# Norms in the scale of later units, projections first, stage ends tile by tile, and gathers for two experts at once, in a two-layer trunk on one core

## The chip, the cores and the metric

One core of one Trainium2 chip. Its engines: TensorE (PE) with its weight loads (PEld), VectorE (DVE), ScalarE (ACT), GpSimd (POOL), SyncE (SP), which issues the DMAs here. The metric is the device time of one execution in microseconds, lower is better.

## The reference, cut to what matters

256 tokens of 1024 float32 values pass two layers. Each layer adds a token mixer and a channel mixer, each behind a root-mean-square norm with a gain; a last norm follows.

```python
h = rmsnorm(x, ln_attn[l])            # x * rsqrt(mean(x*x) + 1e-6) * gain
x = x + token_mixer(h, ...)           # concat[ attention | conv | retention ] @ w_out
h = rmsnorm(x, ln_ffn[l])
x = x + swiglu(h, w13, w2)            # layer 0: (silu(h@A) * (h@B)) @ w2, D_FF = 2816
x = x + moe_ffn(h, router, w13, w2)   # layer 1: top 2 of 8 experts, each such a swiglu
out = rmsnorm(x, ln_final)
```

The token mixer projects h to 2840 columns: queries, keys and values of a three-branch attention (compressed, selected, window; 8 heads of 64), its gates, a 31-tap causal convolution of 256 channels, and a retention of 4 heads. With 256 tokens all blocks are selected, so the selected and the window branch are causal attention over all keys.

## The kernel before, in words

Tokens lie on the partitions in two tiles of 128 (`i` = 0, 1); x stays in SBUF. Weights come through a ring of three slots (`SLOTS`, 24 KB per partition each) by SP, in a fixed order: eight items per mixer, then 11 items of the dense swiglu or 88 of the experts (8 experts x 11 steps of 256 hidden columns). SP waits, before each, until the slot's last reader is done (`LAST_READ`), and its DMAs go out in program order. Each engine runs its own straight program; semaphores order them. The PSUM has eight banks; in a mixer they are handed out in turn by `GROUP`, and `full` and `freed` wait for a bank's use.

**Norm** (`rms_squares` L884, `rms_apply` L1133). ACT squares both tiles with row sums, DVE makes mean + eps, ACT takes the root, DVE the reciprocal and x times it (`xn`), PE transposes `xn` in 16 blocks, DVE multiplies the gain in while copying to `hT`. All that follows waits for it. It comes five times: twice per layer, once at the end.

**Mixer** (`MIXER` L81; the order that PE, ACT and DVE all follow). After the norm: q, ks (window and selected keys), kcv (compressed), vsw (values and gates), cg and ca (convolution gate and input), rqk and rvg (retention). Each projection stage is 16 fp32 matmuls of 128x128 by 256 (32 instructions) or as much in other shape. They stand between the twelve attention units: score k, then probT of k-1 (four transposes), then pv of k-2. For a score DVE takes the row maximum, ACT the exponential; ACT copies probT; DVE scales pv. Other stages in between: conv 0 to 7 (DVE multiply-adds of about four taps each), hid, hidT, cmpkv, cscore, cprobT, cpv (compressed branch), retT, rets, reto (retention). At the end: attn_sum (DVE adds the branches), convT with the layer norm on DVE, retnorm, convB, conv_pw, retcat, and the output product in four groups of (column half, tile): "out" has the first 4 of 8 row blocks, "out_rest" the others; DVE adds each to x.

**Swiglu in three products** (`three`). Each fp32 operand is split in a high part in fp32r (ACT copy, `hi_up`, `hi_down`) and a low rest (DVE subtraction, `lo_up`, `lo_down`), and three matmuls of 512 columns are summed. Per step: four weight pieces for up (`up`), two for down (`down`). Step J: up pieces 0 and 1, turn of step J-1 (transposes of the gated hidden values), up 2 and 3, down of J-1. `hidden` is silu on ACT and the product on DVE, `turned` the split of the transposed values. One buffer holds the four up and two down pieces (`wh`, `wl`), so a piece is split again when PE has read it.

**Experts.** Per expert: `picks` makes a 0/1 matrix token x slot on DVE; `gather` multiplies x (three bf16 parts, 48 matmuls of 128 columns) with it, `picked` scales by the gain and splits (8 ACT and 8 DVE operations), 11 steps, `summed` splits the result, `pick_turned` and `scatter` bring it back to the tokens, `scattered` adds it to x with the gate (4 DVE operations). For expert e > 0 gather stands in step 7 of the expert before, picked in step 10; of the expert before, summed and scatter in step 1, scattered in step 2. Ahead stand the router's logits, `routing` (rank and choice) and the bf16 parts of x. A second round exists for over 128 tokens of an expert, behind a branch; it does not run with this input. After the branch the last norm and the output follow.

Of the kernel before, what the change touches and what calls it, by code (L numbers as in the profile page):

```python
# [7 lines left out]
F32 = mybir.dt.float32  # L8
# [7 lines left out]
P = 128  # L16
# [32 lines left out]
MIX_FILLS = [len([m for m in range(len(MIX_ITEMS)) if m % SLOTS == s]) for s in range(SLOTS)]  # L49
ROUND = EXPERTS * STEPS  # L50


def fills(steps, s):

    return len(range(s, steps, SLOTS))
# [15 lines left out]
for _name, _n in (("ln_attn", KD), ("ln_ffn", KD), ("pe", 2 * 16), ("conv_w", NC * CONV_K), ("conv_b", NC),  # L71
# [10 lines left out]
    ("norm", 0), ("q", 0), ("q", 1), ("ks", 0), ("score", 0), ("kcv", 0), ("score", 1), ("probT", 0), ("vsw", 0),  # L82
    ("score", 2), ("probT", 1), ("pv", 0), ("cg", 0), ("score", 3), ("probT", 2), ("pv", 1), ("ca", 0),
    ("conv", 0), ("score", 4), ("probT", 3), ("pv", 2), ("rqk", 0), ("conv", 1), ("score", 5), ("probT", 4),
    ("pv", 3), ("rqk", 1), ("conv", 2), ("score", 6), ("probT", 5), ("pv", 4), ("hid", 0), ("conv", 3), ("retT", 0),
    ("score", 7), ("probT", 6), ("pv", 5), ("hid", 1), ("conv", 4), ("retT", 1), ("hidT", 0), ("score", 8),
    ("probT", 7), ("pv", 6), ("rvg", 0), ("conv", 5), ("hidT", 1), ("rets", 0), ("score", 9),
    ("probT", 8), ("pv", 7), ("cmpkv", 0), ("conv", 6), ("cscore", 0), ("score", 10), ("rvg", 1), ("probT", 9),
    ("pv", 8), ("rets", 1), ("score", 11), ("probT", 10), ("pv", 9), ("conv", 7), ("cprobT", 0),
    ("probT", 11), ("pv", 10), ("reto", 0), ("pv", 11), ("cpv", 0), ("cpv", 1), ("attn_sum", 0), ("attn_sum", 1),  # L90
    ("convT", 0), ("out", 0), ("retnorm", 0), ("convB", 0), ("out", 1), ("retcat", 0), ("conv_pw", 0),
    ("out_rest", 0), ("out_rest", 1), ("norm", 1)]


PSUM_GROUPS = {"norm": 4, "q": 1, "ks": 1, "score": 1, "kcv": 1, "cg": 1, "ca": 1, "probT": 1, "vsw": 2, "pv": 1,
               "rqk": 1, "rvg": 1, "hid": 1, "hidT": 1, "cmpkv": 1, "retT": 1, "cscore": 2, "rets": 2,
               "cprobT": 1, "reto": 1, "cpv": 1, "convT": 1, "convB": 1, "attn_sum": 1, "conv_pw": 1, "retcat": 1, "out": 2,
               "conv": 0, "retnorm": 0, "out_rest": 0}
BANKS = 8
SCATTER = ((6, 7), (2, 3))  # L100

# [1529 lines left out]
```

## Time and profile before

| | |
|---|---|
| median of 3 runs | 1409.85 us (1407.54 to 1415.88) |
| span of the profiled execution | 1413.9 us (the profile has no other time for it) |
| PE busy | 1317.7 us (93%), 6346 matmuls |
| DVE busy | 989.8 us (70%) |
| ACT busy | 841.6 us (60%) |
| POOL busy | 0.2 us |
| mean DMA rate | 253 GB/s over the span, 337 to 365 in the experts |
| chain of waits | 84% PE, 10% DVE, 3% ACT |

Stages by the timeline: first norm to 15.5, mixer 0 to 185.3, norm to 202, dense swiglu to 394.7, sum and norm to 406.6, mixer 1 to 571, norm and routing to 602, experts to 1397.7, end 1413.9. Times count from the first instruction. An fp32 matmul is two instructions in the profile. The granted clock of PE is 1.00 at 2.4 GHz and 0.50 at 1.2 GHz.

### The profile page before, as it was taken

The numbers are of one execution on the slowest core, as the hardware profiler recorded it, in microseconds if no ns is written. First come the engines' busy times: TensorE is split into PE (matmuls) and PEld (weight loads), VectorE is DVE, ScalarE is ACT, GpSimd is POOL, SyncE is SP. The second block draws the span as 40 slices with busy tenths as digits, with TensorE's granted clock in tenths as the row PEclk, the third lists the DMA queues.
The fourth block names the chain that finished last, engine by engine and source line by source line (L and its number), as shares of the span: only waits on it lengthen the run. The fifth ranks groups of instructions, "written<-read, shape, count | busy, mean of one in ns | idle before, by whom it ended". The sixth has DMA issues, their size and how long they took to land.

```text
span 1413.9 us, 15866 instructions
## 1 busy us (share of the span) xinstructions
PE 1317.7 (93%) x6346; PEld 1056.7 (75%) x6346; DVE 989.8 (70%) x1115; ACT 841.6 (60%) x1181; POOL 0.2 (0%) x4
## 2 busy tenths in 40 slices
PE   6999969999879999699999999999999999999994
PEld 5876548888768764578888888888788788888883
DVE  2275445455322674588898998998998988989993
ACT  2324235444213252387877877887887778778782
POOL 0000000000000000000000000000000000000000
PEclk9998979999979999699999999999999999999998
DMA  8231184552232311769889889989898898898860
GB/s 328 89 133 40 79 327 179 186 197 94 101 140 90 133 62 65 320 249 379 321 352 373 336 350 347 361 342 351 341 369 344 330 385 325 353 380 332 338 263 32
DMA packets 32176, 357.63 MB, mean 253 GB/s; under 512 B 3681, under 2 KB 3809, under 8 KB 4705
## 3 DMA queue, kind: packets, MB, share of 16 engines
q1 hardware_dynamic: 32096, 356.55, 64.4%
q8 instruction: 52, 0.85, 0.2%
q14 instruction: 28, 0.22, 0.0%
HBM read 355.49 MB, written 1.05 MB: 252 GB/s over the span
## 4 chain that ended last, share of the span: by engine, by line
PE 84%; DVE 10%; ACT 3%; issue 1%; DMA 0%; DVEq 0%; ACTq 0%
PE ps L480 81%; DVE wl L1356 4%; PE ps L483 3%; DVE x L1480 1%; DVE hTl L1459 1%; ACT xn L888 1%; ACT wh L1000 1%; ACT hTh L1057 1%; DVE arena L1159 0%; ACT L890 0%; DMA x<-x_in 0%; ACT arena L932 0%; DVE arena L1370 0%; DVE wl L1363 0%; DVE xn L1140 0%
## 5 line engine op out<-in xcount | busy, mean ns | idle before, releaser
L1356 DVE TENSOR_TENSOR wl<-ring,wh 128x2048 fp32r<-128x2048 f32 x198 | 452.9, 2288 | 57.7 <-ACT wh L1000 50.4
L1000 ACT ACTIVATE wh<-ring 128x1024 fp32r<-128x1024 f32 x396 | 419.5, 1061 | 79.1 <-PE ps L480 74.5
L480 PE MATMUL ps<-wh,hTh 128*128 128x512 f32 x880 | 352.6, 401 | 15.2 <-DVE wl L1356 7.6
L480 PE MATMUL ps<-wh,hTl 128*128 128x512 f32 x880 | 345.3, 392 | 0.0
L480 PE MATMUL ps<-wl,hTh 128*128 128x512 f32 x880 | 344.6, 392 | 0.0
L1363 DVE TENSOR_TENSOR wl<-ring,wh 128x2048 fp32r<-128x2048 f32 x99 | 226.6, 2288 | 70.0 <-ACT wh L1010 68.5
L1010 ACT ACTIVATE wh<-ring 128x1024 fp32r<-128x1024 f32 x198 | 209.5, 1066 | 87.1 <-PE ps L480 82.3
L480 PEld LDWEIGHTS ps<-wh,hTh 128*128 128x128 f32 x880 | 165.9, 189 | 51.5 <-DVE hTl L1387 8.0
L480 PEld LDWEIGHTS ps<-wh,hTl 128*128 128x128 f32 x880 | 165.6, 188 | 35.5
L480 PEld LDWEIGHTS ps<-wl,hTh 128*128 128x128 f32 x880 | 166.1, 189 | 32.5
L480 PE MATMUL ps<-wh,gTh 128*128 128x512 f32 x440 | 174.3, 396 | 7.5 <-DVE gTl L1377 7.5
L480 PE MATMUL ps<-wh,gTl 128*128 128x512 f32 x440 | 172.3, 392 | 0.0
L480 PE MATMUL ps<-wl,gTh 128*128 128x512 f32 x440 | 172.2, 391 | 0.0
L480 PEld LDWEIGHTS ps<-wh,gTh 128*128 128x128 f32 x440 | 83.4, 190 | 24.7 <-DVE wl L1363 7.9
L480 PEld LDWEIGHTS ps<-wh,gTl 128*128 128x128 f32 x440 | 83.2, 189 | 17.7
L480 PEld LDWEIGHTS ps<-wl,gTh 128*128 128x128 f32 x440 | 83.5, 190 | 16.8
L480 PE MATMUL ps<-hT,ring 128*128 128x256 f32 x384 | 86.8, 387 | 2.0 <-DVE hT L1184 2.0
L932 ACT ACTIVATE arena<-ps,arena 128x128 f32<-128x128 f32 (+1 forms) x64 | 26.2, 418 | 98.7 <-DVE arena L1224 97.9
L480 PEld LDWEIGHTS ps<-hT,ring 128*128 128x128 f32 x384 | 73.9, 194 | 12.9 <-issue 2.8
L483 PE MATMUL ps<-cst,arena 128*128 128x128 f32 x376 | 65.0, 278 | 10.6 <-ACT arena L932 6.4
L480 PE MATMUL ps<-ring,hT 128*128 128x256 f32 (+2 forms) x256 | 74.1, 447 | 0.0
L1025 ACT ACTIVATE gTh<-ps 128x256 fp32r<-128x256 f32 x110 | 41.6, 388 | 54.6 <-PE ps L483 54.6
(160 smaller groups left out, 1004.6 us busy)
## 6 DMA issues: line engine op xcount, KB each, us to landing
ring<-moe_in SPq DMA_DIRECT2D x88, 2048.0 KB, 8.7
ring<-moe_in SPq DMA_DIRECT2D x88, 1024.0 KB, 8.7
ring<-ffn_in SPq DMA_DIRECT2D x11, 2048.0 KB, 7.5
ring<-mix_in SPq DMA_DIRECT2D x6, 3072.0 KB, 10.1
ring<-ffn_in SPq DMA_DIRECT2D x11, 1024.0 KB, 7.2
ring<-mix_in SPq DMA_DIRECT2D x4, 2048.0 KB, 10.7
ring<-mix_in SPq DMA_DIRECT2D x2, 2368.0 KB, 9.1
ring<-mix_in SPq DMA_DIRECT2D x2, 2176.0 KB, 8.5
```

Of the source, the lines that this page charges most:

```text
L480: return nc.tensor.matmul(o, lhsT, rhs, start=first, stop=last, skip_group_check=True)
L483: return nc.tensor.transpose(o, a, ident)
L888: A(xn[:, i, :], x[:, i, :], ACT.Square, accum_out=stat[:, 0, i:i + 1]).then_inc(s_ss, 1)
L932: last = A(prob[:, k % 3, c * keys:(c + 1) * keys], bank(l, stage, k)[:, c * keys:(c + 1) * keys], ACT.Exp, bias=nmax[:, k, c:c + 1], scal ...
L1000: A(wh[:, p, :], ring[:, J % SLOTS, p * PIECE:(p + 1) * PIECE], ACT.Copy).then_inc(s_hi, 1)
L1010: A(wh[:, UP + c, :], ring[:, J % SLOTS, (UP + c) * PIECE:(UP + c + 1) * PIECE], ACT.Copy)\
L1025: A(gTh[:, i, :, :], ps[:, b, 0:FC].rearrange("p (c t) -> p c t", c=DOWN), ACT.Copy)\
L1057: last = A(hTh[:, c, 0:P], ps[:, 6 + half, q * P:(q + 1) * P], ACT.Copy, scale=param(1, "ln_ffn")[:, c:c + 1])
L1356: V.tensor_tensor(wl[:, w, :], raw, wh[:, w, :].bitcast(F32), ALU.subtract).then_inc(s_lo, 1)
L1363: V.tensor_tensor(wl[:, w, :], raw, wh[:, w, :].bitcast(F32), ALU.subtract).then_inc(s_lo, 1)
L1459: last = V.scalar_tensor_tensor(out=hTl[:, c, 0:P], in0=ps[:, 6 + c // 4, (c % 4) * P:(c % 4 + 1) * P], scalar=param(1, "ln_ffn")[:, c:c + ...
L1480: V.scalar_tensor_tensor(out=xs, in0=ps[:, SCATTER[i][n], :], scalar=gate[:, i, e:e + 1], in1=xs, op0=ALU.mult, op1=ALU.add).then_inc(s_xa ...
```

## The change

- **Dense swiglu's norm goes to the scale of later units.** `hT` for it is transposed from x itself (`xT`, per column half and tile); the factor 1/rms enters as the scale of ACT's silu and of DVE's product in `hidden`. ACT squares (now half tiles, `square`, `root`) run after the mixer, and ACT and DVE wait for the result before dense step 1's pieces. The router's logits come from unscaled x likewise (`logits`), scaled where the softmax is taken.
- **Projections first in a mixer.** The new `MIXER` has stat, nT (norm and transposes per tile), vsw, rqk, rvg, cg, ca, kcv, q, ks ahead of unit 0, with conv 0 to 4 beside them; the twelve units follow with conv 5 to 7 and the rest between. The weight items load in that order (`LOADS`), the first in two DMAs of half. `asum` makes half of each attn_sum earlier; the convolution's layer norm (`cnorm`) comes after both attn_sums.
- **Stage ends tile by tile.** In the mixer's tail `pre` splits the up pieces of the next stage's step 0. The last dense step finishes tile 0 first, sums it, and transposes it between the last products of tile 1; `wh`, `wl` become `whU`, `whD`, `wlU`, `wlD`, and the last step's down pieces go to the up buffers. The end of the experts is done by halves and tiles, in both arms of the branch.
- **Gathers for two experts at once.** x is split in two fp32r parts (ACT, and GpSimd for the rest, no bf16), `pick` is 256 slots wide: 32 matmuls of 256 columns in step 7 of odd experts. picked comes in step 1 (odd) or step 8 (even expert), scatter in step 2, scattered in step 3. `pick_turned` transposes fp32.
- GpSimd also does the memsets. Waits for the low down pieces and for `gTl` stand ahead of each group of three matmuls (`down_part`).

```diff
+    ("stat", 0), ("nT", 0), ("stat", 1), ("vsw", 0), ("nT", 1), ("vsw", 1), ("rqk", 0), ("rqk", 1), ("rvg", 0), ("rvg", 1),
+    ("cg", 0), ("ca", 0), ("conv", 0), ("kcv", 0), ("retT", 0), ("conv", 1), ("q", 0), ("retT", 1), ("conv", 2),
+    ("q", 1), ("conv", 3), ("ks", 0), ("conv", 4),
+    ("score", 0), ("hid", 0), ("score", 1), ("probT", 0), ("rets", 0),
+    ("score", 2), ("probT", 1), ("pv", 0), ("hid", 1), ("conv", 5),
+    ("score", 3), ("probT", 2), ("pv", 1), ("rets", 1), ("hidT", 0), ("hidT", 1),
+    ("score", 4), ("probT", 3), ("pv", 2), ("reto", 0), ("conv", 6),
+    ("score", 5), ("probT", 4), ("pv", 3), ("cmpkv", 0),
+    ("score", 6), ("probT", 5), ("pv", 4), ("cscore", 0), ("conv", 7),
+    ("score", 7), ("probT", 6), ("pv", 5), ("score", 8), ("probT", 7), ("pv", 6), ("cprobT", 0),
...
+    ("asum", 1), ("probT", 11), ("pv", 10), ("convT", 0), ("pv", 11), ("attn_sum", 1), ("cnorm", 0), ("out", 0),
+    ("retnorm", 0), ("convB", 0), ("pre", 0), ("out", 1), ("retcat", 0), ("conv_pw", 0), ("pre", 1),
+    ("out_rest", 0), ("out_rest", 1), ("out_rest", 2), ("xT", 0), ("xT", 1), ("out_rest", 3), ("xT", 2), ("xT", 3)]
...
+                J = STEPS - 1
+                for c in range(DOWN):
+                    for n in range(2):
+                        down_part(DENSE, J - 1, 0, c, n)
+                turn(DENSE, J)
+                for n in range(2):
+                    last = down_part(DENSE, J - 1, 1, 0, n)
+                last.then_inc(s_piece, 1)
+                for n in range(2):
+                    for c in range(DOWN):
+                        last = down_part(DENSE, J, 0, c, n)
+                    last.then_inc(s_ysum, 1)
+                for n in range(2):
+                    last = down_part(DENSE, J - 1, 1, 1, n)
+                last.then_inc(s_piece, 1)
+                for n in range(2):
+                    for c in range(DOWN):
+                        last = down_part(DENSE, J, 1, c, n)
+                    last.then_inc(s_ysum, 1)
+                    if n == 0:
+                        norm_turned(1, 0)
...
+            def down_part(f, J, i, c, n):
+                pe.wait_ge(s_lo, f.down_pair(J) + 1)
+                pe.wait_ge(s_gTl, f.unit(J, i) + 1)
+                w = slice(n * 512, (n + 1) * 512)
+                return three(ps[:, 4 + 2 * i + n, :], g_high(f, J, i)[:, c, :], g_low(f, J, i)[:, c, :], ...)
...
+                for c in range(KD):
+                    b = GATHER[c // 2]
+                    for i in range(NT):
+                        if ex == 0:
+                            pe.wait_ge(s_xl, i + 1)
+                        for part, src in enumerate((xh, xl)):
+                            last = mm(ps[:, b, (c % 2) * 2 * P:(c % 2 + 1) * 2 * P], src[:, i, c * P:(c + 1) * P],
+                                      pick[:, i, :], i == part == 0, i == NT - 1 and part == 1)
...
+                    A(silu[:, i, :], ps[:, up_bank(f, J, i), 0:FC], ACT.Silu,
+                      scale=stat[:, 3, i:i + 1] if f is DENSE else 1.0).then_inc(s_silu, 1)
...
+            for i in range(NT):
+                pool.wait_ge(s_xh, i + 1)
+                if i:
+                    pool.wait_ge(s_xl, i)
+                G.tensor_tensor(xl[:, i, :], xn[:, i, :], xh[:, i, :].bitcast(F32), ALU.subtract).then_inc(s_xl, 1)
```

## Rows read from the trace of the kernel before

**Rows 1.** Windows: stretch, length, busy by engine (instructions), PE clock, DMA share, GB/s.
```profile
15.50:98.90 83.40, 80.91 (x440) 69.82 (x440) 27.61 (x76) 19.24 (x50) 0.00 (x0) 1.00 0.42 165
98.90:185.30 86.40, 80.05 (x358) 48.18 (x358) 46.47 (x120) 30.80 (x69) 0.00 (x0) 0.90 0.20 75
185.30:202.00 16.70, 3.67 (x16) 3.27 (x16) 11.92 (x15) 9.65 (x14) 0.00 (x0) 0.62 0.96 391
...
406.60:492.00 85.40, 83.09 (x440) 71.36 (x440) 27.43 (x75) 19.22 (x49) 0.00 (x0) 0.97 0.24 88
492.00:572.00 80.00, 72.22 (x358) 43.77 (x358) 47.18 (x121) 30.70 (x70) 0.00 (x0) 1.00 0.22 84
...
698.60:797.50 98.90, 98.03 (x478) 80.33 (x477) 88.67 (x72) 78.75 (x100) 0.00 (x0) 1.00 0.90 351
```

**Rows 2.** Chain of work that ended last: start, length in us, what.
```profile
0.73 5.28 DMA x<-x_in
...
15.55 20.97 PE ps L480 x96
...
65.90 8.78 PE ps L480 x45
...
202.02 18.60 PE ps L480 x72
221.06 16.37 PE ps L480 x72
...
372.26 10.94 PE ps L480 x48
...
557.09 13.98 PE ps L480 x32
...
675.17 8.21 PE ps L480 x36
...
709.53 10.03 PE ps L480 x44
...
1401.41 2.78 issue
```

**Rows 3.** Timeline of DVE in mixer 1: start, length, line, operation, [idle before].
```profile
513.20 3.62 DVE L1159 SCALAR_TENSOR_TENSOR arena<-hc,par,arena 128x256 f32<-128x256 f32 x8
516.86 0.61 DVE L1268 SCALAR_TENSOR_TENSOR arena<-ps,cst 128x64 f32<-128x64 f32 x4
...
520.57 0.68 DVE L1222 TENSOR_REDUCE arena<-ps 128x2 f32<-128x512 f32 x1
```

**Rows 4.** Timeline of PE in both mixers.
```profile
100.53 1.08 PE L483 MATMUL ps<-cst,arena 128*128 128x128 f32 x4 [2.59 <-ACT arena L932]
...
493.81 0.63 PE L483 MATMUL ps<-cst,arena 128*128 128x128 f32 x4 [2.59 <-ACT arena L932]
...
538.36 1.06 PE L483 MATMUL ps<-cst,arena 128*128 128x128 f32 x8 [0.70 <-DVE arena L1343]
```

**Rows 5.** Timeline of PE from routing to the first expert.
```profile
581.19 6.97 PE L480 MATMUL ps<-router,hT 128*128 128x8 f32 x32 [0.87 <-DVE hT L1184]
...
597.58 5.03 PE L480 MATMUL ps<-pick,xb 128*128 128x128 bf16 x48 [4.26 <-DVE pick L1450]
...
602.41 0.47 PE L480 MATMUL ps<-wh,hTh 128*128 128x512 f32 x1
```

**Rows 6.** Timeline of PE and DVE in the second expert's stretch.
```profile
666.55 2.85 PE L480 MATMUL ps<-pick,xb 128*128 128x128 bf16 x48
...
696.02 2.16 DVE L1459 SCALAR_TENSOR_TENSOR hTl<-ps,par,hTh 128x128 fp32r<-128x128 f32 x8 [0.29 <-ACT hTh L1057]
...
723.39 2.72 DVE L1480 SCALAR_TENSOR_TENSOR x<-ps,arena,x 128x512 f32<-128x512 f32 x4
```

**Rows 7.** Timeline of PE and DVE at the end.
```profile
1391.02 0.76 PE L480 MATMUL ps<-wh,gTh 128*128 128x512 f32 x1 [3.68 <-DVE gTl L1377]
...
1408.18 2.48 DVE L1144 SCALAR_TENSOR_TENSOR xn<-x,stat,gfin 128x1024 f32<-128x1024 f32 x2
```

More of the change, by code:

```diff
@@ L81 @@
 MIXER = [
[L82 to L91, printed above, removed]
@@ L1094, in experts, with final, final_norm @@
                         A(pickT, ps[:, 3, 0:T].rearrange("p (i t) -> p i t", i=NT), ACT.Copy).then_inc(s_sptc, 1)
-                    hi_down(f, J, 0)
-                    hi_down(f, J, 1)
-                turned(f, ROUND - 1)
-                summed(f, first + EXPERTS - 1)
+                    if j == 8 and ex % 2 and e < EXPERTS - 1:
+                        picked(ex + 1)
+                    if not last:
+                        hi_down(f, J, 0)
+                        hi_down(f, J, 1)
+                turned(f, ROUND - 1)
+            def final(rnd):
+                f = MOE[rnd]
+                ex = rnd * EXPERTS + EXPERTS - 1
+                act.wait_ge(s_yhalf, rnd + 1)
+                A(yeh[:, 0, :], ps[:, 4, :], ACT.Copy).then_inc(s_yeh, 1)
+                act.wait_ge(s_piece, f.end())
+                A(yeh[:, 1, :], ps[:, 5, :], ACT.Copy).then_inc(s_yeh, 1)
+            def final_norm(rnd):
+                ex = rnd * EXPERTS + EXPERTS - 1
+                for i in range(NT):
+                    for h in range(2):
+                        act.wait_ge(s_xadd, 4 * ex + 1 + 2 * i + h + 1)
+                        square(4, i, h)
+                    root(4, i)
             mixer(0)
@@ L1388, in dense @@
+                for i in range(NT):
+                    rstd(1, i).then_inc(s_rstd, 1)
+                dve.wait_ge(s_rstd, NT)
                 for J in range(STEPS):
@@ L1495, in experts @@
                     ex = first + e
+                    last = J == ROUND - 1
                     if j == 1 and e:
-                        summed(ex - 1)
+                        for n in range(2):
+                            summed(ex - 1, n)
                     if J:
                         turned(f, J - 1)
-                    if J < ROUND - 1:
+                    if not last:
                         lo_up(f, J + 1, 0)
-                    if j == 2 and e:
-                        scattered(ex - 1)
@@ L1504, in experts @@
-                    if j == STEPS - 1 and e < EXPERTS - 1:
+                    if j == 3 and e:
+                        for n in range(2):
+                            for i in range(NT):
+                                scattered(ex - 1, i, n)
+                    hidden(f, J)
+                    if not last:
+                        lo_up(f, J + 1, 1)
+                    if j == 1 and ex % 2 == 0:
                         picked(ex + 1)
-                    hidden(f, J)
-                    if J < ROUND - 1:
-                        lo_up(f, J + 1, 1)
```

1040 lines of the change are left out of this document (617 added, 423 removed).

## The prediction

> **What bounds the kernel now.** Read the windows first [rows 1]: in every stage TensorE (PE) is busy nearly all the time, in one expert's stretch 98.03 of 98.90 us, at full clock. What is left is in three places: the stretches between stages (185.3 to 202, some 20 us before 406.6, 571 to 602, and the end), the low clock behind each of them, and some 9 to 10 us of idle PE inside each mixer (83.40 - 80.91 + 86.40 - 80.05 = 8.8 us in layer 0, 2.3 + 7.8 = 10.1 us in layer 1). The chain of waits second [rows 2]: it is PE almost throughout, and it leaves PE only at those boundaries, where it goes through the norm (ACT squares, square root, VectorE (DVE) scaling, transposes, DVE copies). The timelines third [rows 3 to 7]: they give the durations. So the change can gain at boundaries, lose inside the mixers, and touch the expert loop only by the gathers and by where DVE's extra work falls.
>
> The profile has no time of its own for the profiled execution beyond its span, 1413.9 us; the three timed runs are 1407.5 to 1415.9, median 1409.85. I sum against 1413.9 and take off 4.05 at the end.
>
> **Start.** Now x (1 MB) lands at 6.0 (0.73 + 5.28 [rows 2]), norm and transposes of both tiles follow, and the first projection starts at 15.55. New: half of x goes first. About 2 us of the 5.28 are latency, so tile 0 is there at about 4.3; squares 1.4, table load and square root 1.5, reciprocal and scaling 1.0, eight transposes 1.9 with the first copy under them, last copy 0.8: the first projection starts near 10.95. It needs only half of the first weight item (1 MB in place of 3 MB). Tile 1's transposes and copy (1.1 + 1.0) now lie after it. Net 15.55 - 10.95 - 2.1 = **2.5 gained** (bounds 0 to 5). Later weight items come in the order of use; each projection stage is 6.99 us (20.97 / 3), so none is late.
>
> **Inside a mixer.** The PE work is the same. Before, projections (7 us each) stood between the attention units, so a unit's reduce, exp and copy were always covered: 8.78 us for 45 matmuls at 65.90 [rows 2] is one projection and most of a unit, which alone costs PE about 2.2 us. Now all projections come first, and the twelve units run back to back, with DVE also doing the last convolution parts (3.62 each [rows 3]). I walked the new order. Worst place: cscore, conv 7, score 7. DVE's cscore takes 3.7 us (516.86 to 520.57), conv 7 3.6, the reduce of unit 7 0.9 and its exp 1.0: 9.1 us after PE finished cscore, and PE has only score 7, probT 6, pv 5, score 8 in front of probT 7, about 3.3 us: 5.8 idle. Before, rvg (7 us) covered it. Next: conv 4 ahead of unit 0's reduce 1.9, conv 6 1.6, unit 3 0.3, the copy of the keys 1.5 (as before), the sums and copies ahead of "out" 3.5 (before 2.7 to 3.4, since half of the sum is now done early), 0.8 in "out". Together 16 us idle against 8.8 and 10.1. An idle of 5.8 us is longer than those behind which the clock fell: after 2.59 of waiting PE went on at full clock at 493.81 in layer 1 and at half at 100.53 in layer 0 (four transposes 0.63 and 1.08 [rows 4]). That shows in rows 1: the same 358 matmuls are busy 80.05 us at a granted 0.90 in layer 0 and 72.22 at 1.00 in layer 1, 7.8 us for nothing. I charge 2 us per mixer for the clock. Layer 0: -7.2 - 2 + 7.8 = **-1.4**. Layer 1: -5.9 - 2 = **-7.9**. Bounds: idle as before (+14 in all) to another 8 each (-16).
>
> **First mixer to dense.** Before: PE's last output matmul ends at 185.3, the dense ups start at 202.02: 16.7 us with 3.67 of transposes [rows 1], and then 72 matmuls take 18.60 in place of 16.37 [rows 2] from a granted clock of 0.5 (1.2 of 2.4 GHz; the mean over the gap is 0.62). New: the squares and the root are off this path (the scale enters after the up matmuls), weight pieces of step 0 are split during "out", and x is transposed raw, half by half: transposes 2.1 in all, 0.3 of waiting. Half 1's low part is ready 3 us behind the first up, which has 5.5 us of half 0 first. 16.7 - 2.4 + 2.2 = **16.5**. What is late next: ACT does four squares, roots and a wait before it splits step 1; its first DVE piece is ready about 10.1 us after the first up and wanted at 10.9. That cover is 0.8 us; if it is gone, it costs 1 to 3.
>
> **Dense to second mixer.** The last ups end at 377.4 (half of the 48 matmuls from 372.26 [rows 2]); the projections start at 406.6, and their matmuls are 83.09 busy where layer 0's equal 440 are 80.91: 29.2 + 2.2 = 31.4. New: the last down weights are split into the up buffers, so the wait for DVE at 384 to 387 goes; the order is 12 matmuls, turn 0.5, 6, 12, 6, 6, then transposes of tile 0 between the last two groups. At 0.228 each these 48 matmuls take 10.9; sum, squares, root and scaling of tile 0 (4.2 us after its second half) end at 387.8, 0.3 late; vsw of tile 0 starts at 390.3, and tile 1 (1.1 + 0.9) follows. 31.4 - 12.9 - 2.0 = **16.5**.
>
> **Second mixer to experts.** Before: 571.07 to 602.41, 31.3 us. New, from the last output matmul: two first logit halves 2.1, transposes 1.0, copy, two second halves 2.0, so logits at 5.5 in place of 17 (the old 32 took 6.97 at half clock [rows 5]). Selection 2.2 (fewer links), rank 0.5 in bf16, DVE's leftovers and the rank copy 0.9, four picks of 0.3: gather at 9.9. PE is idle most of 5.5 to 9.9, so its clock will be low: the old first gather ran 48 in 5.03 [rows 5] at half clock, against 2.85 later, and the clock rose about at its end. The new one has 32 matmuls of 256 columns: 0.213 each at half clock for 5 us, 0.13 for the rest, 6.1. First up at 16.0, plus 1.06 for the two earlier transposes: **14.2 gained** (bounds 9 to 18). GpSimd's two subtractions have no row in this trace: DVE's equal one is 1.22; up to 3.8 for the second is hidden, since its input is there at 6.1 and the picks end at 9.9. I take 2.4, twice DVE; at 6 us it would cost 2.2. By the Trainium skill, GPSIMD Engine Reference, Engine selection, a two-input elementwise operation should not go to GpSimd, about 2x slower; its 4497 ns for 2048 columns would make this an estimate of 2.2 us, still hidden. No row here shows it.
>
> **Expert loop.** Before, from 602.41 to the last ups: per expert 98.9 [rows 1], made of 11 x 8.434, gather 2.8 (48 matmuls [rows 6]), scatter 1.82 (10.03 - 8.21 [rows 2]), pick transposes 0.19, stalls 1.3. New: three gathers in the loop of 32 matmuls in place of seven of 48. The pace of a matmul with 128 fp32 weight columns is 0.13 us (8 in 1.06 [rows 4]), above the 0.107 that 256 columns stream: 4.1 each. 19.6 - 12.3 = 7.3. Bounds for it: 0.114 (half of the 512-column pace) to 0.218 (fp32): +1.5 to -8.5. Here the Trainium skill (TensorE: Matmul & The Clock Gate, Weight-path perf modes) speaks against the change: fast weight load is for weights that aren't fp32, so the gather gives it up; its load time of 107 ns is an estimate of 3.4 per gather, 2 us better in all than my 4.1. Pick transposes in fp32: -0.6. Stalls: DVE's pieces are 7.7 of each 8.43, and its results are some 1.9 us ahead of need, so an inserted piece stalls PE by what goes over 1.9. Before, picked (2.16 [rows 6]) at the last step, summed (1.3) and scattered (2.72) within three steps: 1.3 per expert. New, even experts: summed and picked at step 1, 0.8; scattered at step 3, 1.3; odd ones about 0.1: 1.1 per expert. In all 11.7 to 8, 3.6. Sum **10.3** (bounds 0 to 15). DMA: a step wants 3.15 MB per 8.43 us, 373 GB/s, windows reach over 400; no bound.
>
> **The end.** Before, the last down starts at 1391.02 at half clock (0.76 the first) behind 3.68 idle [rows 7], and 1401.41 to 1404.2 is the branch [rows 2]; then norm and output of both tiles. New: last down weights split early, down at 1387.9 at full clock, ends 1390.7; the branch (about 3.4 on ACT and DVE) runs beside it; yeh and yel by halves to 1393.0, scatter, four sums to 1395.9, tile 0's norm beside them, last product at 1400.1, output 3.2 (1413.9 less the last product's end, 1410.7 [rows 7]). Ends at 1403.3: **10.6** (bounds 6 to 13).
>
> **Sum.** 2.5 - 1.4 + 16.5 + 16.5 - 7.9 + 14.2 + 10.3 + 10.6 = 61.3. 1413.9 - 61.3 - 4.05 = 1348.5; the forecast is **1348**.
>
> **Rivals.** (A) Forecast, 1348, own range 1338 to 1358. (B) The mixer's units stay covered: idle as before, clock kept, 14 less: 1334. For it: the page's DVE is busy only 27.6 of 83.4 us in the first half of a mixer; against: the count at cscore. (C) The opposite: twelve bare units, each with reduce, exp and copy in series, wait 0.7 more each, or the gather runs at the fp32 pace: 16 or 9 more, 1357 to 1370. (D) The norm work is not hidden but moved: ACT's squares hold up dense step 1, and the first expert steps wait for DVE, so two of the three boundary gains are halved: 1365. (E) Slower: the down matmuls now carry two waits for each three matmuls. That is 6 more per expert step and 14 more per dense step, 88 x 6 + 11 x 14 = 682. From 0.09 us each the gain is gone; at 0.12, 1430. Against: 36 matmuls with six met waits take 8.21, 72 with six take 16.37, the same pace, so a met wait costs under 0.01.
>
> **Chances.** A 0.50, B 0.20, C 0.17, D 0.08, E 0.03, 0.02 for something between. Range 1328 to 1371: B and most of C and D lie in it. A measurement of this kernel tells 0.5% (7 us) from no change. Faster 0.96, same 0.01, slower 0.03.
>
> **What would show it.** Dense ups at about 185 and at full clock; second mixer's first projection near 371, first expert up near 560; one PE idle of 5 to 6 us behind cscore in each mixer; 32-matmul gathers of about 4 us every other expert; the last down at full clock with no idle before it. I am wrong if the clock stays low in the bare units, if PE waits at dense step 1 by more than 3 us, or if a pair of experts isn't 1.5 to 3 us shorter than 197.8.

## The result and the profile after

The changed kernel takes 1376.63 us (median of 4 runs, 1375.6 to 1380.82), the kernel before 1411.03 us on the same chip (1407.54 to 1415.88): ratio 0.976, 95% interval 0.973 to 0.978. It is faster by 34 us, where 61 were forecast, and lies 5.6 us above the range. The profiled execution of after is its slowest run, 1380.82 us with a span of 1379.0; the span of before is 1413.9, so the two traces differ by 34.9 us.

The first fence is the timeline of TensorE (PE) after (start, length, line, shapes, count, in brackets the idle time before and who ended it); it holds the marks that the prediction named at the stage boundaries.

```profile
199.71 0.48 PE L555 MATMUL ps<-whU,hTh 128*128 128x512 f32 x1
386.75 4.01 PE L555 MATMUL ps<-ring,hT 128*128 128x280 f32 x16 [0.40 <-PE ps L555]
535.62 9.96 PE L555 MATMUL ps<-ring,arena 128*128 128x512 f32 x16 [0.73 <-issue]
580.85 0.21 PE L555 MATMUL ps<-selb,beforeb 128*128 128x8 bf16 x2 [5.26 <-DVE selb L1670]
582.75 0.58 PE L555 MATMUL ps<-pick,xh 128*128 128x256 f32 x1 [1.60 <-DVE pick L1695]
```

With these starts and those of before, each stage can be set against the prediction's terms. The terms are its own, put together by stage; of the 7.8 us of low clock that it takes back from before in layer 0, 1.2 are counted in "out", whose first 16 matmuls took 8.30 us there in place of 7.1. Their sum is its 61.3.

| stretch | before | after | measured | predicted |
|---|---|---|---|---|
| start to "out" of layer 0 | 152.65 | 163.20 | +10.6 | +0.1 |
| "out" to first dense up | 49.4 | 36.5 | -12.9 | -15.5 |
| dense, to the second mixer's first projection | 204.6 | 187.0 | -17.5 | -18.7 |
| second mixer to its "out" | 133.1 | 148.9 | +15.7 | +7.9 |
| "out" to first expert up | 62.7 | 52.3 | -10.4 | -14.2 |
| experts and end | 811.5 | 791.1 | -20.4 | -20.9 |
| sum | | | -34.9 | -61.3 |

The reader is to see that boundaries, experts and end came within about 1.5 us each, leaving aside "out", and that the two mixers and their "out" hold 24.2 of the missing 26.4 us. Windows over the mixers say how (length, busy time of PE, weight loads, DVE, ACT and POOL with instructions, granted clock of PE, share of the DMAs, GB/s). Before, first projection to "out", both layers:

```profile
15.55:152.65 137.10, 129.21 (x719) 103.20 (x719) 62.78 (x172) 44.93 (x111) 0.00 (x0) 0.95 0.34 133
406.59:539.72 133.13, 124.76 (x718) 100.87 (x719) 62.97 (x173) 44.71 (x111) 0.00 (x0) 0.98 0.24 91
```

After, the same stretches, then the unit phases alone:

```profile
11.13:163.20 152.07, 137.65 (x726) 111.90 (x727) 67.14 (x183) 37.52 (x107) 0.00 (x0) 0.91 0.37 148
386.75:535.62 148.87, 134.10 (x727) 109.74 (x727) 66.90 (x182) 38.28 (x109) 0.00 (x0) 0.92 0.25 95
99.00:163.20 64.20, 52.40 (x344) 45.35 (x345) 37.52 (x111) 28.01 (x89) 0.00 (x0) 0.78 0.19 76
468.00:535.60 67.60, 55.33 (x390) 47.39 (x391) 41.76 (x120) 28.02 (x89) 0.00 (x0) 0.82 0.24 94
```

Idle time of PE rose from 7.9 and 8.4 us to 14.4 and 14.8 (length less busy). The busy time of nearly the same work rose by 8.4 and 9.3 us, only 1.04 of it for the eight transposes of tile 1 that moved into the stretch. The granted clock of the unit phase is 0.78 and 0.82, a mix of 1.2 and 2.4 GHz, where layer 1 before had 1.00 [rows 1]. (At the very start of an execution the column is no guide: layer 0's first 16 matmuls after take 6.28 us where layer 1's take 4.01, and the clock shown there is 1.00.) The timeline of layer 1's units shows where the clock fell:

```profile
492.83 1.05 PE L555 MATMUL ps<-arena 128*128 128x128 f32 x8
496.16 0.63 PE L558 MATMUL ps<-cst,arena 128*128 128x128 f32 x4 [2.28 <-ACT arena L1084]
496.93 5.41 PE L555 MATMUL ps<-arena 128*128 128x64 f32 x40
502.46 1.92 PE L555 MATMUL ps<-arena 128*128 128x256 f32 x4
...
511.71 1.09 PE L558 MATMUL ps<-cst,arena 128*128 128x128 f32 x4 [3.64 <-ACT arena L1084]
527.05 1.32 PE L558 MATMUL ps<-cst,arena 128*128 128x128 f32 x8 [1.48 <-DVE arena L1561]
533.79 1.09 PE L558 MATMUL ps<-cst,arena 128*128 128x128 f32 x4 [1.37 <-DVE arena L1561]
545.86 7.03 PE L555 MATMUL ps<-ring,arena 128*128 128x512 f32 x16
```

Four transposes take 0.63 us at full clock and 1.09 at half: behind the wait of 2.28 they are still fast, the 40 short matmuls that follow are not (5.41 us; 2.97 at full clock in the run with dummies at two waits), nor the scores (four in 1.92 instead of 1.03) and the transposes behind 3.64. Windows from 496 on place the fall about a microsecond behind the end of the wait:

```profile
496.00:496.80 0.80, 0.63 (x4) 0.42 (x4) 0.80 (x2) 0.62 (x2) 0.00 (x0) 1.00 0.94 369
496.80:498.00 1.20, 1.07 (x6) 1.10 (x6) 0.59 (x4) 0.77 (x5) 0.00 (x0) 0.58 0.99 423
498.00:500.00 2.00, 2.00 (x16) 1.88 (x17) 0.29 (x1) 1.34 (x6) 0.00 (x0) 0.50 1.07 451
500.00:502.30 2.30, 2.30 (x23) 2.26 (x24) 0.00 (x0) 0.00 (x0) 0.00 (x0) 0.50 0.95 406
```

It is back at full for units 9 to 11 and lost again at the sums. "Out" itself, long matmuls without a gap, takes 9.96 us for its first 16 and 7.03 for the next. In layer 0 the same first 16 take 10.14. The DVE timeline beneath the longest wait (cscore, the eighth part of the convolution, then unit 7's reduce):

```profile
502.37 0.61 DVE L1484 SCALAR_TENSOR_TENSOR arena<-ps,cst 128x64 f32<-128x64 f32 x4 [3.16 <-PE ps L555]
...
506.08 3.63 DVE L1381 SCALAR_TENSOR_TENSOR arena<-hc,par,arena 128x256 f32<-128x256 f32 x8
509.62 0.68 DVE L1439 TENSOR_REDUCE arena<-ps 128x2 f32<-128x512 f32 x1
```

PE finishes cscore at 502.3 and is released at 511.7, 9.4 us later; the prediction had 9.1. So the walk through the new order was right. What was not is the pace at which PE works beside it.

### The profile page after: what moved, and what is told of

The parts are those of the page before. It is cut to its first block, busy times and chain, and to the rows that moved or that the text cites. A ratio compares the mean times of both kernels' runs of the same rounds, so it can differ in the third digit from the quotient of the medians.

```text
span 1379.0 us, 15726 instructions
## 1 busy us (share of the span) xinstructions
PE 1314.9 (95%) x6085; PEld 1054.9 (76%) x6085; DVE 986.9 (72%) x1117; ACT 830.7 (60%) x1194; POOL 8.5 (1%) x12
## 3 DMA queue, kind: packets, MB, share of 16 engines
HBM read 355.49 MB, written 1.05 MB: 259 GB/s over the span
## 4 chain that ended last, share of the span: by engine, by line
PE 87%; DVE 9%; ACT 2%; issue 1%; DMA 0%; DVEq 0%; ACTq 0%
PE ps L555 83%; PE ps L558 4%; DVE wlU L1593 3%; DVE x L1723 1%; DVE arena L1381 1%; ACT arena L1084 1%; ACT whU L1170 1%; DVE arena L1439 0%; DVE wlD L1600 0%; DVE xn L1357 0%; DMA x<-x_in 0%; DVE arena L1561 0%; DVE arena L1408 0%; DVE hT L1365 0%; ACT gTh L1196 0%
## 5 line engine op out<-in xcount | busy, mean ns | idle before, releaser
L1593 DVE TENSOR_TENSOR wlU<-ring,whU 128x2048 fp32r<-128x2048 f32 x198 | 453.2, 2289 | 75.6 <-ACT whU L1170 72.2
L1170 ACT ACTIVATE whU<-ring 128x1024 fp32r<-128x1024 f32 x396 | 418.5, 1061 | 65.2 <-PE ps L555 60.7
L555 PE MATMUL ps<-whU,hTh 128*128 128x512 f32 x880 | 352.8, 401 | 4.2 <-DVE wlU L1593 4.2
L555 PE MATMUL ps<-whU,hTl 128*128 128x512 f32 x880 | 344.9, 392 | 0.0
L555 PE MATMUL ps<-wlU,hTh 128*128 128x512 f32 x880 | 343.1, 390 | 0.0
L1600 DVE TENSOR_TENSOR wlD<-ring,whD 128x2048 fp32r<-128x2048 f32 x97 | 222.1, 2289 | 51.7 <-ACT whD L1182 51.7
L1182 ACT ACTIVATE whD<-ring 128x1024 fp32r<-128x1024 f32 x194 | 205.3, 1065 | 74.9 <-PE ps L555 69.5
L555 PE MATMUL ps<-whD,gTh 128*128 128x512 f32 x428 | 168.1, 393 | 0.4 <-DVE gTl L1618 0.4
L555 PE MATMUL ps<-whD,gTl 128*128 128x512 f32 x428 | 167.4, 391 | 0.0
L555 PE MATMUL ps<-wlD,gTh 128*128 128x512 f32 x428 | 166.6, 389 | 0.0
L558 PEld LDWEIGHTS ps<-cst,arena 128*128 128x128 f32 x376 | 52.3, 151 | 41.3 <-issue 26.9
L555 PEld LDWEIGHTS ps<-hT,ring 128*128 128x128 f32 x384 | 72.6, 190 | 10.6 <-issue 1.0
```

The costliest lines, as they stand in the source:

```text
L555: return nc.tensor.matmul(o, lhsT, rhs, start=first, stop=last, skip_group_check=True)
L558: return nc.tensor.transpose(o, a, ident)
L1170: A(whU[:, p, :], ring[:, f.slot(J), p * PIECE:(p + 1) * PIECE], ACT.Copy).then_inc(s_hi, 1)
L1182: A(wh_down(f, J, c), ring[:, f.slot(J), (UP + c) * PIECE:(UP + c + 1) * PIECE], ACT.Copy)\
L1593: V.tensor_tensor(wlU[:, w, :], raw, whU[:, w, :].bitcast(F32), ALU.subtract).then_inc(s_lo, 1)
L1600: V.tensor_tensor(wl_down(f, J), raw, high.bitcast(F32), ALU.subtract).then_inc(s_lo, 1)
```

## The experiments

Theory 1: the mixers lose by the clock, which falls because PE waits between short units. Theory 2: they lose by the idle time itself, or the clock is low for the shape of the units' matmuls. Rivals: another part of the change. Times are medians of 4 runs (of 10 for the last one); "mixers" are the times from first projection to "out" in layer 0 and 1 of the profiled execution.

**Dummies in the waits.**

```diff
+ def spin(o, n):
+     for _ in range(n):
+         mm(o[:, 0:512].rearrange("p (n k) -> p n k", n=4), identb[:], spread(causalb[:], 1, 4), True, True)
  elif stage == "probT":
      o = begin(l, stage, k)
+     spin(o, {0: 8, 5: 9, 7: 15}.get(k, 0))      # and 6, 6, 5, 2 at score 0, the sums, out
      pe.wait_ge(s_exp, l * len(UNITS) + k + 1)
```

> The kernel after, with dummy bf16 matmuls of 512 columns (0.21 us each at full clock) put on TensorE just ahead of the waits of the unit phase: 6 ahead of unit 0's scores, 8, 9 and 15 ahead of the turns of units 0, 5 and 7, 6 and 5 ahead of the two attention sums, 2 ahead of the output projection (51 per mixer, each group no longer than the idle time it stands in; what they write is overwritten). Nothing else moves. Theory 1 (the loss in the mixers is mostly the clock: TensorE waits with nothing to do, then goes on at half clock; against before 8.5 and 9.3 us of the 15.0 and 15.7 are longer busy time): the granted clock from the first unit to the end of 'out' stays near 1.00, the two mixers take about 143 and 140 us in place of 152 and 149, the whole 1359 to 1363. Theory 2 (the loss is the idle time itself, and the clock is low there because the units' matmuls are narrow, whatever stands between them): the dummies change nothing or run at half clock themselves and overrun the gaps: 1377 to 1390.

Measured: 1360.21 us (1358.32 to 1360.75), ratio to before 0.962 (0.959 to 0.966); mixers 144.21 and 141.67. Its PE timeline at the end of layer 1's units, and its unit phase in a window:

```profile
516.27 0.66 PE L558 MATMUL ps<-cst,arena 128*128 128x128 f32 x4 [0.20 <-DVE arena L1570]
517.66 7.11 PE L555 MATMUL ps<-ring,arena 128*128 128x512 f32 x16 [0.30 <-issue]
457.45:517.66 60.21, 58.38 (x435) 44.85 (x436) 41.09 (x118) 27.80 (x89) 0.00 (x0) 0.94 0.27 107
```

No real work moved, and 16.4 us are gone from the median; "out" is at full clock. Between the two traces it is 21.0 us: the mixers stand 7.9 and 7.2 us lower, each "out" 3.0 and 2.9. So most of the loss is the clock, as theory 1 says, and filled waits keep it up. But the clock of the unit phase is 0.94 and not near 1.00, and the stretch that is left has no long wait ahead of it:

```profile
486.10 3.47 PE L555 MATMUL ps<-arena 128*128 128x64 f32 x40 [0.20 <-ACT arena L1103]
489.69 1.92 PE L555 MATMUL ps<-arena 128*128 128x256 f32 x4
```

From about 488.4 to 495.2 PE runs at half clock (the four scores in 1.92 us instead of 1.03), though in the 24 us before it waited only 0.24 and 0.20 us. In layer 0 the same happens at the same place, from about 126.6 on. The fall comes among the 40 short matmuls of the first row, which are 8 of 64 columns and then cscore's 32 of 16 columns; in the next run the same 40, behind the same dummies, stay at full clock in layer 1. So waits are not the only thing that brings the clock down, and whether short matmuls do it alone was not isolated.

**Dummies at two of the waits only** (9 and 15, units 5 and 7).

> The kernel after with 9 and 15 dummies ahead of the turns of units 5 and 7 only (2.28 and 3.64 us of waiting), none elsewhere. With dummies in all seven waits the whole fell by 17 us. If the clock is lost at these two waits only: nearly the same, 1360 to 1364. If any wait between short units costs it, it falls later, at the two sums ahead of 'out' (1.48 and 1.37 us), and the 16 matmuls of 'out' take about 10 us instead of 7.1: 1366 to 1370. If the two waits have nothing to do with it: 1377.

Measured: 1370.77 us (1363.27 to 1372.33), ratio 0.969 (0.965 to 0.974); mixers 146.08 and 146.38.

```profile
504.01 0.66 PE L558 MATMUL ps<-cst,arena 128*128 128x128 f32 x4 [2.71 <-ACT arena L1093]
517.03 1.94 PE L558 MATMUL ps<-cst,arena 128*128 128x128 f32 x8 [1.47 <-DVE arena L1570]
526.32 9.04 PE L555 MATMUL ps<-ring,arena 128*128 128x512 f32 x16 [0.84 <-issue]
```

The whole is 0.8 us above the second expectation. Units 5 to 9 keep the full clock, and it falls at the sums instead: eight transposes 1.94 us, "out" 9.04. Filling two of the waits gave 5.9 us of the 16.4. The row at 504.01 gives the idle of unit 7 at full clock: 15 dummies of 0.213 us and 2.71 are 5.9 us, the prediction's 5.8. After showed 3.64 only because PE worked at half clock through the 9.4 us of DVE and ACT, so part of the slow work lay where it would have waited.

**The old order of projections and units**, with its loads, in the new kernel.

```diff
- ("vsw", 0), ("nT", 1), ("vsw", 1), ("rqk", 0), ... ("q", 1), ("ks", 0), ("score", 0), ...
+ ("q", 0), ("q", 1), ("ks", 0), ("score", 0), ("kcv", 0), ("score", 1), ("probT", 0), ("vsw", 0), ...
- LOADS = ((2, ...), (3, ...), (1, ...), (0, ...), ...
+ LOADS = ((0, ...), (1, ...), (2, ...), (3, ...), ...
```

> The kernel after, with one part undone: inside the mixers the projections stand between the attention units again in the order of the kernel before (q first, so the first projection needs both token tiles), and the weight items are loaded in that order; the new boundaries, the norm after the up matmuls, the expert loop and the end stay. Theories 1 and 2 alike (the loss comes from the bare units): first projection to output projection takes 134 to 138 us in each mixer in place of 152.1 and 148.9, with the clock at 1.00 in layer 1; the boundaries ahead of the mixers lose 2 to 3 us each; whole 1350 to 1354. Rival (the loss comes from something else that the change brought into the mixers, as the split sums, the waits on banks or the loading of weights): the mixers stay near 149 to 152, whole 1377 to 1383.

Measured: 1369.22 us (1367.38 to 1372.02), ratio 0.969 (0.965 to 0.972); mixers 142.57 and 142.05. A miss of 15 us: half of the loss came back. It had kept the new end of the units, with the products of the compressed branch right behind their transposes. So that end was undone too:

```diff
- ("cpv", 0), ("cpv", 1), ("probT", 11), ("pv", 10), ("asum", 0), ("reto", 0), ("attn_sum", 0), ("asum", 1),
- ("convT", 0), ("pv", 11), ("attn_sum", 1),
+ ("probT", 11), ("pv", 10), ("reto", 0), ("pv", 11), ("cpv", 0), ("cpv", 1), ("asum", 0), ("asum", 1),
+ ("attn_sum", 0), ("attn_sum", 1), ("convT", 0),
```

> The kernel with the projections between the units again (the earlier run with the old order took 142 us in each mixer, not 134 to 138), now with the end of the units too in the order of the kernel before: products of units 10 and 11, then the sums of both tiles one after the other, then the transposes of the convolution. If the missing 7 us of that run came from its split sums (waits of 1.68, 1.67, 1.37 and 0.73 us, and the half clock behind them): mixers at 134 to 137, whole 1355 to 1360. If they came from elsewhere (the bare vsw stages ahead, the loads, the banks): no change, 1367 to 1371.

Measured: 1356.56 us (1356.42 to 1362.22), ratio 0.962 (0.957 to 0.967); mixers 133.25 and 138.11. Windows of the two kernels, layer 0, the first with the new end, the second with the old:

```profile
15.43:158.00 142.57, 132.07 (x718) 105.85 (x719) 64.67 (x178) 42.47 (x110) 0.00 (x0) 0.94 0.36 142
```

```profile
15.46:148.71 133.25, 124.70 (x718) 100.80 (x719) 63.23 (x175) 42.17 (x110) 0.00 (x0) 1.00 0.39 153
```

The same 718 matmuls are busy 132.07 and 124.70 us. The second is nearly the price of a mixer's work at full clock; only its first 96 matmuls took 23.12 us where layer 0 before took 20.96 (20.97 in [rows 2]), so the price is 122.5, and layer 1 before gives the same (124.76 less the 2.2 us of its slow first 96). The two steps bring 20.1 us together, 13 of them the second. But not all of the 13 is the order of the sums: in layer 0 the kernel with the new end had already lost 5.4 us to the other by cprobT, the last stage that both have in the same place, and 1.7 us in layer 1, over the same instructions and waits; its clock fell behind the wait of 2.60 in layer 0, the other's did not. Of the 9.3 and 3.9 us by which the mixers differ, 4.0 and 2.3 come behind the first stage that was moved. The rest is where the clock happened to fall.

**The convolution under the projections.** Here the projections stay first and the units bare; DVE's convolution leaves the unit phase, and for that cg and ca, with their weight item, come ahead of rqk.

```diff
- ("vsw", 1), ("rqk", 0), ("rqk", 1), ("rvg", 0), ("rvg", 1), ("cg", 0), ("ca", 0), ("conv", 0), ("kcv", 0), ...
+ ("vsw", 1), ("cg", 0), ("ca", 0), ("rqk", 0), ("conv", 0), ("rqk", 1), ("conv", 1), ("rvg", 0), ("conv", 2),
+ ("rvg", 1), ("conv", 3), ("retT", 0), ("kcv", 0), ("conv", 4), ... ("q", 1), ("conv", 6), ("conv", 7), ("ks", 0),
```

> The kernel after, with cg and ca moved ahead of rqk (and their weight item loaded second), so that all eight convolution parts run on VectorE under the projections and none in the unit phase. The projections still come first and the units still run bare. Theory 2 (VectorE's order makes the idle): the waits of TensorE for the exp of units 0, 5 and 7 (1.96, 2.28 and 3.64 us in layer 1) fall below 1 us each, 5 to 6 us of idle less in each mixer; if the clock then still falls in the units: 1364 to 1367. Theory 1 (it is the waits that bring the clock down): with fewer waits the clock stays up too and another 5 to 8 us per mixer come back: 1350 to 1356. Rival (each bare unit is a series of reduce, exp and copy that takes longer than TensorE's part of it): idle only moves from unit to unit, 1372 to 1378.

Measured: 1348.77 us (1347.94 to 1352.32), ratio 0.955 (0.952 to 0.959), 1.2 us below the range for theory 1. Its mixers:

```profile
11.15:145.24 134.09, 126.88 (x727) 102.98 (x727) 67.19 (x182) 37.43 (x107) 0.00 (x0) 0.99 0.42 167
367.25:503.94 136.69, 127.38 (x726) 104.12 (x727) 67.45 (x182) 38.31 (x109) 0.00 (x0) 0.96 0.27 104
```

Against after it is 27.9 us in the medians; in the traces 7.2 and 5.5 us less idle, 10.8 and 6.7 less busy for the same matmuls. The waits at the turns of units 0 and 5 are gone, that of unit 7 is 0.84 in layer 0 and 2.50 in layer 1:

```profile
126.67 0.63 PE L558 MATMUL ps<-cst,arena 128*128 128x128 f32 x4 [0.84 <-ACT arena L1084]
480.96 0.63 PE L558 MATMUL ps<-cst,arena 128*128 128x128 f32 x4 [2.50 <-ACT arena L1084]
```

The two are one and the same release. DVE and ACT let PE go 10.06 and 10.05 us after the start of unit 6's scores (116.61 and 470.91). In layer 0 the clock had fallen at about 121, and PE's own work ahead of the wait took longer (four scores 1.87 us, four transposes 1.06; in layer 1 1.03 and 0.60), which is the 1.66 us by which the wait is shorter. So half clock ahead of this wait costs nothing, since PE would have waited anyway. That fall, too, came with no wait since 94.39, right behind the same 40 short matmuls as in the run with dummies.

The bare units are thus no great fault by themselves: most of the clock is lost where PE waits, and DVE's order made the waits. What is left is at the sums (waits of 1.48 and 1.37) with "out" at 8.59 and 10.14 us.

**On top of it, one edit each.** The end of the units reordered, so that the convolution's transposes stand in the last wait:

```diff
- ("pv", 9), ("attn_sum", 0), ("asum", 1), ("probT", 11), ("pv", 10), ("convT", 0), ("pv", 11), ("attn_sum", 1),
+ ("pv", 9), ("asum", 1), ("probT", 11), ("pv", 10), ("pv", 11), ("attn_sum", 0), ("convT", 0), ("attn_sum", 1),
```

> The kernel with the convolution early, and one more edit: the products of units 10 and 11 come first, then the attention sum of tile 0, the transposes of the convolution (0.85 us), the sum of tile 1. If the waits of 1.48 and 1.37 us ahead of 'out' are real dependences that other work can cover: the first goes, the second falls to about 0.5, 2.4 us per mixer, and 'out' runs at full clock (7.1 in place of 8.6 and 10.1 us): 1338 to 1343. Rival: VectorE still works on units 10 and 11 whatever stands there, the waits only move: 1347 to 1350.

Measured: 1342.31 us (1340.77 to 1343.43), ratio 0.951 (0.946 to 0.955); mixers 133.44 and 134.77.

```profile
497.64 1.50 PE L558 MATMUL ps<-cst,arena 128*128 128x128 f32 x12 [1.14 <-DVE arena L1561]
499.88 7.11 PE L555 MATMUL ps<-ring,arena 128*128 128x512 f32 x16 [0.73 <-issue]
```

One wait of 1.14 us and one under 0.5 in place of 1.48 and 1.37, and "out" at full clock. Dummies in the remaining waits instead:

> The kernel with the convolution early, plus dummies of 0.21 us: 6 ahead of unit 0's scores, 4 ahead of unit 7's turn, 6 and 5 ahead of the two sums, 2 ahead of 'out' (23 per mixer, about 4.9 us, in gaps of 1.53, 0.84 or 2.50, 1.48, 1.37 and 0.73). Theory 1 (waits bring the clock down): the last stretches at half clock go, 1.5 us in layer 0 and 3 to 4 in layer 1, whole 1343 to 1346. If the clock is only lost in waits over 2 us: nothing, 1348 to 1350.

Measured: 1342.05 us (1339.56 to 1343.89), ratio 0.951 (0.946 to 0.955); mixers 134.14 and 132.42, "out" 7.1 in both. It gains slightly more than expected and as much as the reordering, which costs nothing. Among the waits that it filled only the one of 2.50 us was longer than 2, and in layer 0 there was none such, yet "out" came back to full clock there too: the waits of 1.48, 1.37 and 0.73 us ahead of it matter.

The end, with the branch's condition and the table for the square root loaded ahead:

```diff
+ act.wait_ge(s_over, 1)
+ more = act.value_load(over[0:1, 0:1], min_val=0, max_val=1)
  experts(0)
+ act.preload_act_table(ACT.Sqrt)
```

> The kernel with the convolution early, and the end changed: ScalarE and VectorE load the branch's condition before the experts, and the table for the square root is loaded ahead of the branch. After the last transposed unit the chain of the kernel after has 2.45 us of branch and 1.28 of table load on ScalarE, beside 4.3 us of last down matmuls. If that ScalarE chain ends last: 1 to 3 us less, 1346 to 1348, and the copy of the first half follows the down matmuls at once. If the branch alone takes the 2.45: 1.3 us less at most. If the down matmuls end last anyway: no change, 1349.

Measured: 1347.21 us (1343.79 to 1347.95), ratio 0.953 (0.949 to 0.958). The chain of waits of its end:

```profile
1328.17 0.42 DVE arena L1611
1328.60 1.25 DVE wlU L1600
1330.71 0.43 DVE gTlY L1618
1331.28 3.00 PE ps L555 x12
1334.30 0.61 ACT yeh L1297
```

The branch and the table load have left the chain, but from the last up matmul to the end it is 18.4 us here (1327.73 to 1346.1) and without the edit (1328.1 to 1346.5). DVE's split of the last down weights now ends last. By its number this is the first outcome, by its trace the third: the end got no shorter. The traces differ in layer 1's mixer (134.68 for 136.69), which no edit touched, and the 1.5 us between the medians can't be put down to the edit. All orders together, with no dummies:

> Orders alone, no dummies: convolution early, the new end of the units (units 10 and 11, sum 0, convolution transposes, sum 1) and the branch's condition and table loaded ahead. The gains of the three runs add if they are in different places: 1342.3 - 1.6 gives 1340 to 1341. If one only moves a wait into another: 1342 to 1345.

Measured: 1343.16 us (1341.67 to 1343.23), ratio 0.951 (0.948 to 0.954). The second outcome; the median is 0.9 us above the kernel with the new end of the units alone, within the spread of both. Unit 7 waits 2.50 us in layer 0 too, where that kernel waited 0.85. PE is again released at the same distance, here with the clock at full until the wait and fallen behind it (scores of 128 columns in 1.91 us instead of 1.05), there the other way round; from unit 7's turn to "out" it is 19.41 us here and 17.77 there.

**The fastest version**, the same orders with 19 dummies per mixer in the waits that are left, and 28 around the selection:

```diff
+ spin(ps[:, 5, :], 22)
  pe.wait_ge(s_sel, 1)
```

> The same, plus dummies where TensorE still waits: 6 ahead of unit 0's scores, 6 ahead of unit 7's turn, 1 and 4 ahead of the sums, 2 ahead of 'out', 22 ahead of the selection and 6 ahead of the first gather. The half clock in the last units of layer 1 (about 2 us) and in the first 14 to 25 matmuls of the first gather (1.5 to 2.5 us) goes: 1336 to 1338. If the dummies in the selection hold up the rank matmuls or slow VectorE: 1340 or more.

Measured: 1340.67 us (1340.01 to 1340.92), ratio 0.949 (0.947 to 0.952); mixers 134.21 and 132.26. In the selection the dummies fill PE, and the first gather starts at full clock:

```profile
536.26 7.31 PE L555 MATMUL ps<-causalb,identb 128*128 128x512 bf16 x22
543.41 0.20 PE L555 MATMUL ps<-selb,beforeb 128*128 128x8 bf16 x2
...
545.10 0.38 PE L555 MATMUL ps<-pick,xh 128*128 128x256 f32 x1
545.32 0.28 PE L555 MATMUL ps<-pick,xl 128*128 128x256 f32 x1
```

0.117 us a matmul from the third on, where after spent 0.213 on about 13 of the 32. But the whole is 2.7 us above the expected range's upper end, and the expectation's other branch came true: the dummies held up the rank. VectorE had the selection ready at 540.7, and PE, still at its dummies (22 in 7.3 us, so partly at half clock), began the rank matmuls at 543.41. From the second logit half to the first up it is 15.4 us here and 14.4 in the kernel without dummies (533.53 to 548.96, 537.09 to 551.53). So what is gained, 2.5 us to that kernel and 1.6 to the one with the new end of the units alone, comes from the mixers, not from the selection.

**Dummies in the kernel before**, 10 at unit 6's turn.

```diff
  elif stage == "probT":
      o = begin(l, stage, k)
+     if k == 6:
+         spin(o, 10)
```

> The kernel before, with 10 of the same dummy matmuls ahead of the wait of unit 6's turn, where TensorE idles 2.59 us in both layers and then went on at half clock in layer 0 alone. Theory 1: layer 0's unit phase loses its stretch at half clock, 7 to 8 us less (1403 to 1404), layer 1 is as it was. Theory 2: no change, or up to 2 us more: 1411 to 1413.

Measured: 1413.27 us (1409.38 to 1415.08), ratio 1.001 (0.999 to 1.002): no change that the runs can tell (3 us would not show), where theory 1 as I had put it asked for 7 to 8. Layer 0 of its trace, and the same "rvg" in the trace of the kernel before:

```profile
101.94 0.66 PE L483 MATMUL ps<-cst,arena 128*128 128x128 f32 x4 [0.34 <-ACT arena L938]
124.53 8.73 PE L480 MATMUL ps<-ring,hT 128*128 128x512 f32 x16
149.85 8.16 PE L480 MATMUL ps<-ring,arena 128*128 128x512 f32 x16
```

```profile
127.17 9.02 PE L480 MATMUL ps<-ring,hT 128*128 128x512 f32 x16
```

The stretch at half clock behind the wait is gone (the four transposes took 1.08 [rows 4]), but the clock still falls later, in rvg (8.73 for 7.09) and in "out" (8.16 for 7.11), behind waits of 0.97, 1.37 and 0.70 us. These falls are not new: before had them too (9.02, and 8.30 in "out"). So the 7.8 us of low clock in layer 0 were three stretches and not one, and the filled wait accounted for only the first of them; from the first projection to "out" layer 0 takes 134.56 us here and 137.10 before.

## Why the prediction was wrong, step by step

- **Inside a mixer: the term that failed, by its clock, not by its idle time.** The walk gave 16 us of idle per mixer (its items add up to 15.4), 0.8 of them in "out"; after has 14.4 and 14.8 ahead of "out" and 0.78 in it. Place by place: unit 0 1.96 (1.9 predicted), unit 5 2.28 (1.6), the keys' copy 1.60 (1.5), sums and copies 3.58 (3.5), unit 7 3.64 (5.8, and 5.9 at full clock). The charge "2 us per mixer for the clock" was the mistake. At full clock the work is 122.5 us, 123.6 with tile 1's transposes; after has 137.65 and 134.10, and 3.0 and 2.9 more in "out": 17.1 and 13.4 us. 2.3 of layer 0's are the first projection (6.28 us at its start for 4.01), which is no matter of the units. That leaves 28.2 where 4 in all were charged, so the term was 24 us too small, of 26.4 missing.
- Why it was charged so low: I took the cost of one wait from before (7.8 us for one of 2.59 in one layer, nothing in the other) and did not ask what a series of waits does. The 7.8 us were themselves three stretches, as the run with dummies in the kernel before shows. After has four at half clock in layer 0 and three in layer 1 from the first unit to the end of "out", among waits of 1.4 to 3.7 us with short matmuls between and no projection (0.78 and 0.82 on the mean). The bounds (+14 to -16 for both mixers together) were set on idle time alone and did not contain the clock.
- The Trainium skill, TensorE: Matmul & The Clock Gate, HAM oscillation, describes kernels whose PE swings between the two clocks since it waits between bursts, there for DMA. This trace agrees, with waits for DVE and ACT: 0.78 and 0.82 in the units. The run with dummies does not quite: its clock fell once per mixer where PE had waited 0.24 us at most.
- **Start.** First projection at 11.13 (10.95 predicted). Right.
- **First mixer to dense.** First up at 199.71, 36.5 us behind "out" where 33.9 were forecast; "out" at half clock has 3.0 us too much. The boundary itself hit: 0.44 us of waiting (0.3). PE did not wait at dense step 1, so that cover of 0.8 us held, and rival D fell.
- **Dense to second mixer.** 17.5 of 18.7 us. Right within 1.2.
- **Second mixer to experts.** 3.8 us short: 2.9 of them in "out". Rank at 580.85, gather at 582.75, first up at 587.95, 17.3 us behind the last output matmul's end where 16.0 were predicted. GpSimd's subtractions, which had no row, took:

```profile
573.65 2.35 POOL L1824 TENSOR_TENSOR xl<-xn,xh 128x1024 fp32r<-128x1024 f32 x1 [198.83 <-ACT xh L1312]
577.72 2.34 POOL L1824 TENSOR_TENSOR xl<-xn,xh 128x1024 fp32r<-128x1024 f32 x1 [1.72 <-ACT xh L1314]
```

  2.4 was taken, and the second ends at 580.06, ahead of the picks: hidden, as predicted.
- **Expert loop and end.** 20.4 of 20.9 us. A gather in the loop:

```profile
747.62 0.28 PE L555 MATMUL ps<-pick,xh 128*128 128x256 f32 x1
...
751.37 0.40 PE L555 MATMUL ps<-whD,gTh 128*128 128x512 f32 x1
```

  32 matmuls in 3.75 us (4.1 predicted), 0.117 each. A pair of experts takes 195.5 us (719.14 to 914.64), 2.3 less than 197.8, within the 1.5 to 3 of the prediction. Rival C's fp32 pace of the gather did not come, and a bare unit did not wait 0.7 us more than walked.
- **Rival E**, the waits in the down matmuls: a dense step takes 16.82 us after and 16.80 before (means of nine), with 14 waits more, so a met wait costs under 0.003 us. It was not tried by a run of its own.
- **Rival B**, the units stay covered, fell with the count at cscore; with the convolution moved (mixers at 134.09 and 136.69) it is nearly true, and 1348.8 us is the forecast's number, by another kernel.
- The sentence "I am wrong if the clock stays low in the bare units" named the right place, and its price was not in the rivals: idle as walked with the clock lost as measured gives 1348 + 24 = 1372.

What stays open: in which execution the clock falls where. The kernel before loses it in the units of layer 0 and not in those of layer 1 (0.90 and 1.00 [rows 1]), with the same instructions and waits, and the kernel with the old order and the old sums the other way round. Each kernel was traced once, so gains of 1 to 5 us in one stage can be such a shift. Open too is why the clock fell among short matmuls with hardly a wait.

## What to carry to other kernels

Where dense matmuls are moved away from short ones and waits recur among these, an estimate of idle time alone is half of the cost: here PE was idle 14.4 and 14.8 us in the mixers and lost another 14.8 and 13.4 to the clock, 3 of them in the first dense work behind the short ones. Then look at the engine that PE waits for: moving 11 us of DVE work out of the unit phase gave back 28 us, though DVE was busy only 58 and 62% of that time. Filling a few waits of a series leaves the others to bring the clock down (two of seven gave 5.9 us of the 16.4, one in the kernel before nothing that the runs can tell); shorten or fill all of them, at best with real work that has no wait of its own (here the transposes of the convolution).

## What the runs showed of the hardware

- The clock can fall with a delay: the four transposes right behind the wait of 2.28 us still ran at full clock (window at 1.00), the matmuls from 497 on, with no gap among them, at half (0.50). Elsewhere the transposes behind the wait are slow at once (1.08 behind 2.59 in layer 0 before [rows 4]). Whoever looks only at the first work behind a wait can miss the fall.
- The clock can fall without a wait: with dummies in the waits it fell in both layers among 40 short matmuls (8 of 64 columns, 32 of 16), with waits of 0.24 us at most in the 24 us before.
- Half clock under another engine's work costs less than its busy time says: at unit 7 it took 2.3 us out of the wait (5.9 to 3.64), and 1.66 of 2.50 with the convolution early.
- fp32r matmuls with 256 moving columns and 128 weight columns follow each other at 0.117 us at full clock and 0.213 at half; 512 columns at 0.228.
- GpSimd subtracts 1024 columns in 2.34 us.
